# One transformer stack on one core: the convolution's tiles placed anew, sums and copies moved by a step, and the beginning in another order

## The reference, cut to what matters

```python
def modulate(h, shift, scale):
    return h * (1.0 + scale) + shift

def adaln(cond, prm):                       # 72 chunks of 1 MB for both layers
    mod = jax.nn.silu(cond) @ prm["mod_w"] + prm["mod_b"]

def half_ffn(x, m, name):
    sh, sc, g = m
    h = modulate(rms_norm_2(x, prm[name + "_norm"]), sh, sc)
    return x + 0.5 * g * swiglu(h, prm[name + "_w_in"], prm[name + "_w_out"])

def conv_module(u, prm):                    # mixer of b2.0, 512 channels, latent and context apart
    a, g = jnp.split(u + prm["conv_glu_b"], 2, axis=-1)
    y = a * jax.nn.sigmoid(g)
    y = depthwise convolution of y over 31 tokens (15 on each side), + conv_dw_b
    return jax.nn.silu(layer_norm(y, prm["conv_ln_g"], prm["conv_ln_b"]))
```

## Time and profile before

| | |
|---|---|
| time, median of 3 runs | 2585.43 us (2583.7 to 2586.07) |
| profiled execution, its own time | 2585.32 us |
| its span | 2583.5 us |
| TensorE busy | 2494.8 us, 97% |
| VectorE, ScalarE, POOL busy | 1330.1, 986.3, 132.2 us |
| TensorE on the chain that ended last | 90% |
| DMA | 353.13 MB, 137 GB/s |

### The profile page before, as it was taken

The page is one execution under the profiler, slowest core; times in us unless marked ns, Lnnn a source line. Parts: engine busy times, 40 slices in busy tenths (PEclk is TensorE's granted clock), DMA queues, the critical chain, the costliest instruction groups (busy, mean ns, idle before and its releaser), DMA issues.

```text
span 2583.5 us, 39883 instructions
## 1 busy us (share of the span) xinstructions
PE 2494.8 (97%) x16458; PEld 2095.1 (81%) x16458; DVE 1330.1 (51%) x1978; ACT 986.3 (38%) x1482; POOL 132.2 (5%) x161
## 2 busy tenths in 40 slices
PE   7999999999899999999999999999999999988999
PEld 6998899998888888876457788887888887857999
DVE  4567775488753333345764543343443343355654
ACT  4346544366462222251263421223321224345532
POOL 0000000000000000002930000000000000011000
PEclk9999999999999999999999999999999999999999
DMA  5447555454342322332541423224222232533553
GB/s 216 174 150 253 173 177 196 141 183 159 131 163 95 125 82 77 110 115 91 212 173 63 150 95 109 90 97 160 96 95 98 88 116 90 188 131 123 184 192 106
DMA packets 62690, 353.13 MB, mean 137 GB/s; under 512 B 14400, under 2 KB 17600, under 8 KB 26432
## 3 DMA queue, kind: packets, MB, share of 16 engines
q1 hardware_dynamic: 62528, 350.82, 38.9%
HBM read 349.75 MB, written 1.05 MB: 136 GB/s over the span
## 4 chain that ended last, share of the span: by engine, by line
PE 90%; DVE 5%; ACT 2%; DMA 2%; issue 1%; POOL 0%; SPq 0%; DVEq 0%; ACTq 0%; POOLq 0%
PE psum L1251 16%; PE psum L1252 16%; PE psum L1253 16%; PE psum L772 11%; PE psum L809 7%; PE psum L811 6%; PE psum L810 6%; DVE slab L2349 2%; PE psum L884 1%; PE psum L890 1%; PE psum L885 1%; PE psum L1140 1%; DVE ring_lo L2217 1%; PE psum L915 1%; PE psum L917 1%
## 5 line engine op out<-in xcount | busy, mean ns | idle before, releaser
L1251 PE MATMUL psum<-h_hi,w_hi 128*128 128x512 f32 (+1 forms) x1408 | 513.2, 364 | 10.0 <-DVE h_lo L2186 7.8
L1252 PE MATMUL psum<-h_lo,w_hi 128*128 128x512 f32 (+1 forms) x1408 | 511.6, 363 | 0.0
L1253 PE MATMUL psum<-h_hi,w_lo 128*128 128x512 f32 (+1 forms) x1408 | 511.5, 363 | 0.0
L2363 DVE TENSOR_TENSOR w_lo<-wring,w_hi 128x1024 fp32r<-128x1024 f32 (+1 forms) x240 | 318.6, 1330 | 305.0 <-ACT w_hi L1791 304.6
L1791 ACT ACTIVATE w_hi<-wring 128x1024 fp32r<-128x1024 f32 (+1 forms) x240 | 273.3, 1143 | 525.8 <-PE psum L1253 518.4
L809 PE MATMUL psum<-h_hi,w_hi 128*128 128x256 f32 (+1 forms) x1176 | 357.0, 304 | 1.9 <-DVE ring_lo L2217 0.9
L811 PE MATMUL psum<-h_hi,ring_lo 128*128 128x256 f32 (+1 forms) x1176 | 348.5, 296 | 0.0
L810 PE MATMUL psum<-h_lo,w_hi 128*128 128x256 f32 (+1 forms) x1176 | 347.9, 296 | 0.0
L2217 DVE TENSOR_TENSOR ring_lo<-wring,w_hi 128x1024 fp32r<-128x1024 f32 x208 | 246.8, 1223 | 167.7 <-ACT w_hi L1670 165.7
L1251 PEld LDWEIGHTS psum<-h_hi,w_hi 128*128 128x128 f32 x1408 | 266.3, 189 | 54.8 <-issue 8.6
L1253 PEld LDWEIGHTS psum<-h_hi,w_lo 128*128 128x128 f32 x1408 | 266.4, 189 | 41.4
(11 more groups left out here) (203 smaller groups left out, 3451.3 us busy)
## 6 DMA issues: line engine op xcount, KB each, us to landing
wring<-in_w_b_ffn_in SPq DMA_DIRECT2D x84, 1024.0 KB, 4.9
wring<-in_w_mod SPq DMA_DIRECT2D x72, 1024.0 KB, 5.1
wring<-in_w_b_ffn_out SPq DMA_DIRECT2D x64, 704.0 KB, 4.0
wring<-in_w_b_merge SPq DMA_DIRECT2D x24, 1024.0 KB, 4.9
wring<-in_w_b_out SPq DMA_DIRECT2D x16, 1024.0 KB, 4.9
wring<-in_w_b_in SPq DMA_DIRECT2D x16, 1024.0 KB, 5.7
wring<-in_w_b_q SPq DMA_DIRECT2D x12, 1024.0 KB, 4.9
wring<-in_w_b_k SPq DMA_DIRECT2D x12, 1024.0 KB, 4.8
```

The costliest lines, as they stand in the source:

```text
L1251: nc.tensor.matmul(acc, wh[:, k, :], rhs_hi[k], start=(k == 0), stop=False)
L1252: nc.tensor.matmul(acc, wh[:, k, :], rhs_lo[k], start=False, stop=False)
L1253: return nc.tensor.matmul(acc, wl[:, k, :], rhs_hi[k], start=False, stop=(k == n - 1))
L2363: V.tensor_tensor(part_piece(w_lo, q, i), raw_piece(c, i), part_piece(w_hi, q, i).bitcast(F32), ALU.subtract).then_inc(weights_split, 1)
```

## The change

It has six parts.

- **Convolution.** TensorE takes tiles 3 and 0. Four copies of a tile's input, shifted by one token each, stand in four groups of 32 partitions, for 32 channels at a time; 16 DMAs from SBUF to SBUF make them for a tile, on SyncE's queue, 32 x 2 x 284 elements each. One product then does four taps of 32 channels: 8 quads of taps by 4 groups of channels, 32 products with 32 output rows and 512 columns. Their weights are an additional 1 MB chunk ("taps"). VectorE takes tiles 2 and 1, one after the other, POOL none; the buffers of the diagonals go. The order of the chunks around it follows.
- **Context.** Squares, sums and root one chunk later.
- **Attention.** The rows are copied a step earlier than now (their turn a step later, in the last one).
- **Beginning.** x first, then constants, then parameters. The table of the root is loaded at once. The first roundings and splits stand behind root and reciprocal, the silu of the condition behind the first roundings of the input.
- **b2.1.** Six modulation chunks with the heads instead of five, two before ffn2 instead of three, those of the attention at steps 2 to 5 instead of 0 to 3, its two splits two steps later.
- **FFN.** The second input chunk has a name of its own in the plan; only before b2.1.ffn2 does it come earlier, behind the first modulation chunk.

```diff
-DVE_CONV, POOL_CONV = 2, 1
-PE_CONV = DVE_CONV + POOL_CONV
 CONV_ORDER = (3, 0, 2, 1)
+PE_CONV, DVE_CONV = CONV_ORDER[0:2], CONV_ORDER[2:4]
+QUADS = (TAPS + 3) // 4
+REACH = SEQ + 4 * (QUADS - 1)
...
-              ("b2.0.heads", 6), ("b2.0.att", 7), ("b2.0.n2", 3), ("b2.1.n1", 5), ("b2.1.nm", 4), ("b2.1.heads", 5), ("b2.1.att", 4),
-              ("b2.1.n2", 3)]
+              ("b2.0.heads", 6), ("b2.0.att", 7), ("b2.0.n2", 3), ("b2.1.n1", 5), ("b2.1.nm", 4), ("b2.1.heads", 6), ("b2.1.att", 4),
...
+SECOND_AT = {"b2.1.n2": 1}
...
-ROUND_AT = {"b1.0": (KD - 1, KD - 1), "b2.0.n1": (0, 0), "b1.1": (KD - 2, KD - 2), "b2.1.n2": (KD - 2, KD - 2)}
...
+ROUND_AT = {"b1.0": (KD, KD), "b2.0.n1": (0, 0), "b1.1": (KD - 2, KD - 2), "b2.1.n2": (KD - 2, KD - 2)}
...
-        out[i * (steps - 3) // len(MODS[nm]) if nm[1] == "1" else i].append(("mod", l, c))
+        out[i * (steps - 3) // len(MODS[nm]) if nm[1] == "1" else i + 2 * (nm == "b2.1.att")].append(("mod", l, c))
     if MODS[nm]:
-        out[steps - 2].append(("turn", 0, 0))
+        out[steps - 2].append(("rows", 0, 0))
+        out[steps - 1].append(("turn", 0, 0))
...
-        for at, c in ((4, 0), (6, 1)):
+        for at, c in ((6, 0), (8, 1)):
...
-        mods(before)
+        chunks = [(f"mod{m}", 1, KD * 256) for m, _ in MODS[before]]
+        at = SECOND_AT.get(before, len(chunks))
+        plan.extend(chunks[:at] + [(f"{nm}_second", 1, KD * 256)] + chunks[at:])
...
-            mods("b2.0.conv")
-            plan += [("b2.0.in", 2, KD * 256)]
+            taps = [(f"mod{m}", 1, KD * 256) for m, _ in MODS["b2.0.conv"]]
+            plan += taps[0:2] + [("b2.0.taps", 1, len(PE_CONV) * QUADS * P)]
+            plan += [("b2.0.in", 2, KD * 256)] + taps[2:]
             between = [("mod%d" % m, 1, KD * 256) for m, _ in MODS["b2.0.uq"]]
-            plan += [("b2.0.uq", 1, 3 * 384)] + between[0:2] + [("b2.0.uq", 1, 3 * 384)] + between[2:5]
-            plan += [("b2.0.ukv", 1, 2 * 1024)] + between[5:7]
+            plan += [("b2.0.uq", 1, 3 * 384)] + between[0:2] + [("b2.0.uq", 1, 3 * 384)] + between[2:4]
+            plan += [("b2.0.ukv", 1, 2 * 1024)] + between[4:7]
             mods("b2.0.heads")
         else:
             between = [(f"mod{m}", 1, KD * 256) for m, _ in MODS["b2.1.heads"]]
-            plan += [("b2.1.in", 7, KD * 256)] + between[0:2] + [("b2.1.in", 1, KD * 256)] + between[2:]
+            plan += [("b2.1.in", 7, KD * 256)] + between[0:3] + [("b2.1.in", 1, KD * 256)] + between[3:]
...
-            sp.dma_start(prm[:, :], d_param).then_inc(s_first, 16)
-            sp.dma_start(cst[:, 0:EARLY], d_const[:, 0:EARLY]).then_inc(s_first, 16)
             for i in range(2):
                 sp.dma_start(x[:, KH_X * i:KH_X * i + KH_X, 0:SEQ], d_x[:, KH_X * i:KH_X * i + KH_X, :]).then_inc(s_x, 16)
+            sp.dma_start(cst[:, 0:EARLY], d_const[:, 0:EARLY]).then_inc(s_first, 16)
+            sp.dma_start(prm[:, :], d_param).then_inc(s_first, 16)
...
+                for n in range(len(PE_CONV)):
+                    if c == start["b2.0.taps"][0] + n:
+                        for ready in ("b2.0.conv.margin", f"b2.0.conv.glu{PE_CONV[n]}"):
+                            if E.new(ready):
+                                sp.wait_ge(*E.at(ready))
+                        for j in range(4):
+                            w = min(REACH, YW - j)
+                            for g in range(GROUPS):
+                                sp.dma_start(m_shifted[n][GW * j:GW * j + GW, g, :, 0:w],
+                                             m_y[GW * g:GW * g + GW, PE_CONV[n], :, j:j + w]).then_inc(s_shift[n], 16)
...
+            def convolve(n, wv, chunk=None):
+
+                acc = take(f"b2.0.conv.pe{n}", fixed=6).rearrange("p (a s) -> p a s", a=2)
+                pe.wait_ge(s_shift[n], 16 * 4 * GROUPS)
+                for k in range(QUADS):
+                    for g in range(GROUPS):
+                        mm = product(acc[GW * g:GW * g + GW, :, :], wv[:, n, k, GW * g:GW * g + GW], m_shifted[n][:, g, :, 4 * k:4 * k + SEQ],
+                                     k, QUADS)
+                if chunk is not None:
+                    E.name_next(f"w{chunk}")
+                mm.then_inc(tap_multiplied, 1)
+                E.step(tap_multiplied, f"b2.0.conv.pe{n}")
...
-                    if l == 1 and j < 2:
-                        for k in range(4 * j, 4 * j + 4):
+                    if l == 1 and j in (1, 2):
+                        for k in range(4 * j - 4, 4 * j):
...
-                    convolve(MODS["b2.0.conv"])
+                    modulation(*MODS["b2.0.conv"][0])
+                    taps, w = state["c"] + 1, slot_of(state["c"] + 1)
+                    wv = w[:, 0:len(PE_CONV) * QUADS * P].rearrange("p (n k c) -> p n k c", n=len(PE_CONV), k=QUADS)
+                    pe.wait_ge(landed[taps % SLOTS], 16 * (taps // SLOTS + 1))
+                    convolve(0, wv)
+                    modulation(*MODS["b2.0.conv"][1])
+                    state["c"] += 1
...
+                if j == 5:
+                    convolve(1, wv, taps)
+                if j == 6:
+                    modulation(*MODS["b2.0.conv"][2])
...
-                A(warm[:, :], C("eps"), ACT.Sqrt).then_inc(rooted, 1)
-                act.wait_ge(rooted, E.step(rooted))
+                if nm == "b1.0":
+                    A(warm[:, :], csil[:, 0, 0:1], ACT.Sqrt).then_inc(rooted, 1)
+                    act.wait_ge(rooted, E.step(rooted))
...
-                if l == 1:
-                    context_squares()
-                for m in range(8, 10):
-                    round_chunk(last[m])
+                for m in range(2):
+                    if l == 1:
+                        context_squares(range(4 * m, 4 * m + 4))
+                    round_chunk(last[8 + m])
+            context_root()
...
+                        if kind == "rows":
+                            copy_rows(nm)
                         if kind == "turn":
-                            copy_rows(nm)
...
-                if ahead and nm in ROUND_AT:
+                if ahead and nm in ROUND_AT and nm != "b1.0":
...
-            for k in range(TAPS):
-                tap(k)
-                if k == 19:
-                    split_chunk(projections[6])
             rope_pieces("b2.0.lora")
-            glu(2)
-            glu(1)
-            for k in range(TAPS):
-                tap(TAPS + k)
+            split_chunk(projections[6])
+            for i in DVE_CONV:
+                glu(i)
+                for k in range(TAPS):
+                    tap(i, k)
```

121 lines of the change are left out of this document (58 added, 63 removed).

## The result

The changed kernel takes 2558.64 us in the median of four runs (2558.06 to 2559.42), the kernel before 2585.75 beside it: 27.1 us less, a ratio of 0.9892 (0.9877 to 0.9907). I had forecast 2553.1, in 2546 to 2566. So the direction and most of the mechanisms held, and 5.1 of 32.2 us did not come. The profiled execution took 2558.64, its span is 2556.6.

A forecast was written before the change was run, and what follows sets the result against it. TensorE was taken as the bound, busy 2494.8 of 2583.5 us. Mixer −17.0, beginning −3.4, context −4.35, rows and turn −2.1 and last layer −5.4 sum to −32.2: 2585.3 to 2553.1 us, range 2546 to 2566.

The forecast's parts named there:

- The convolution on TensorE: Mixer of b2.0: 27.2 us of diagonal products go, 128 overlapping records cost 15.1 (bounds 14.2 and 56.7), saving 12.1.
- VectorE's taps and the reciprocal: Mixer: 60 taps at 0.796 us end about 1253.5, reciprocal at 1254.5, before TensorE needs it at 1262.0; 3.5 us wait goes.
- I give 0.6 back: Mixer: three modulations instead of two stand behind each other before the attention, at the queue's pace, costing 0.6 us.
- The copies at nothing: Mixer: 32 shifted-copy DMAs on SP's queue land in time and cost nothing; TensorE waits under 1 us for them.
- The beginning: Kernel start: x lands about 0.9 us earlier, root ends at 13.8 instead of 18.03; −3.4 us, bounds −1.5 to −4.5.
- The context: Last output chunks: sums one chunk later remove the wait for ScalarE's squares, −4.35 us; up to 2 may come back.
- Rows and turn: Attentions of two layers: row copy a step earlier, turn a step later; 2 × −1.05 = −2.1 us, bounds 0 and −5.2.
- The last layer: b2.1: later modulations in attention −3.5, a sixth at the heads −1.0, before ffn2 −0.9; together −5.4 us.
- rival D: Gains outside the mixer turn into the next wait, half of 15.2 us gone, 2560.7; chance 0.23.
- A: Convolution on TensorE: the groups do not overlap, 128 records take 56.7 us in line, 2594.7; chance 0.03.
- B: Mixer: VectorE becomes the bound, taps of 1.386 us make the reciprocal late by 28, 2581.1; chance 0.04.
- C: Mixer: shifted copies are late, at an issue of 1.0 us; +6 us, 2559.1; chance 0.15.

The follow-up runs named there:

- the groups in line: Changed kernel with the two loops of TensorE's convolution exchanged, all eight quads of one column group before the next group: 2590.49 us, ratio 1.0006.

## Why the prediction was right, and where it was off

- **The convolution on TensorE: right.** 12.1 forecast; two sets of 6.9 instead of 7.55 give 27.2 − 13.7 = 13.5. The longer records lost nothing at all, they are even below my lower bound of 14.2 for both, since a record of this form takes 0.429 in line and not the 0.443 that I took from the diagonal products. The exchanged loops show that the overlap of groups is the reason. At the changes between the widths little is to be seen: around the second set the records start 0.1 us late ahead of it and 0.14 behind it (1197.08; the last four records of the set start at 1196.51, and 0.43 behind them would be 1196.94), near the 0.3 that I left out; whether that is a drain no run shows.
- **VectorE's taps and the reciprocal: right.** Done before TensorE wants it, 0.786 a tap, and slow again as soon as POOL works.
- **"I give 0.6 back" for the chunks at the heads: the term that failed.** 3.8 came back. I had counted the pace of the queue (2.5 us a chunk) and overlooked what stands ahead of it. The chunk ukv holds its slot until 1247.5, and the three modulations behind it theirs, so from 1230.7 to 1247.6 SyncE loads nothing. Before, there was a gap of 19 us too (1255.3 to 1274.2), under the 3.54 of the reciprocal. A stall had hidden a stall: with POOL kept busy the reciprocal is late again, and the waits for chunks are gone. Fewer and later modulations there took them away for good, in two kernels.
- **The copies at nothing:** 1.1 in the first profile and 0.3 in the second, where I had allowed 1. The first set was issued 0.1 behind the GLU and took 10.33 where I had 9.9, and its last copy landed 4.0 later. The load of in5 behind it was not late.
- **The beginning: the mechanism right, x's landing mis-sized.** I took 0.9 for asking first; it is 2.7 at the first product. The rest, 3.5 by the run with constants first, was 2.5 in my sum (3.4 − 0.9). Together they are 6.2, outside my bound of 4.5: the first product starts at 16.31, where I had 19.1.
- **The context: right, and worth 7.25 to 7.5 instead of 4.35**, as TensorE ran the products behind the wait at half its clock in both profiles of before.
- **Rows and turn: right** (1.1 and 0.85 for 1.05 each).
- **The last layer: a size off.** −2.4 to −3.5 for −5.4. The attention gave 1.4 to 1.8 for 3.5, since ScalarE's and POOL's waits took the rest, as rival D had it. The new places ahead of the FFN gave 0.6 or 0.7 for 0.9, and this is no more than the modulation of 1.0 that went to the heads.
- **Not forecast: the clock.** From 1300 to 2240 the changed kernel lost 3.3 to 3.4 us in both profiles, where nothing but the copy of the rows in one attention was moved; 2.7 to 3.0 of it stand at the lower clock.
- **Errors that cancel.** Convolution, context and beginning gave some 6 to 8 us more than forecast, the heads, the copies, the last layer and the stretch from 1300 to 2240 some 10 less. That the sum is only 5.1 off is in part luck.

Of the rivals, A is refuted by the trace, and B did not come because POOL rests; the runs with the groups in line and with POOL kept busy show that both are real where their condition holds. C's condition, an issue of 1.0 us, was not met; the 1.1 came from a late landing. D is what happened in the last layer, and within the mixer, where it had not been looked for, at the heads.

## What to carry to other kernels

Narrow float32 products cost a quarter (0.107 us a record instead of 0.429) if neighbours go to four different column groups, and most of that is lost (0.35) if the same products stand in the other loop order. Before a wait is counted as gain, ask which other wait ends just under it: here a reciprocal's 3.5 us had covered the gap of a ring whose slots one long-lived chunk held. And look at the clock behind a wait before you price it: at the context it made 7.25 of 4.35. The reverse holds as well: waits can look short because TensorE runs slowly under them, as ahead of the last FFN, so time such a place from end to end.

## What the runs showed of the hardware that was not expected

- In each of the 14 profiles TensorE lost 16 to 32 us of engine time in stretches in which its clock stood at the lower of its two levels (0.50 of 2.4 GHz, so 1.2). Some stretches come back at the same work: the one behind the wait at the context in both profiles of the kernel before, and one at the start of the last FFN in eight of nine profiles with its new places and in none of five with those of before. Others move between profiles of one kernel. They do not need a wait in front: in the first profile of the changed kernel the clock fell at 494.3 behind 10 us in which TensorE was busy throughout, and in the second profile it stayed at full speed there.

```profile
484.00:494.00 10.00, 10.00 (x58) 8.72 (x57) 4.44 (x5) 2.98 (x4) 0.00 (x0) 1.00 0.33 124
494.30:501.10 6.80, 6.80 (x26) 5.59 (x26) 4.06 (x10) 3.29 (x5) 0.00 (x0) 0.50 0.47 154
```

  The Trainium skill (TensorE: Matmul & The Clock Gate, Part 1: The HAM clock gate) says of a kernel's start that the count of slow products varies from run to run, since the gate's window runs freely. The profiles agree as far as they show the same kernel with slow stretches in other places, five new and three gone between the first two. What draws a slow stretch stays open.
- A slow stretch costs from nearly all of its lost share to nearly nothing: 1.5 us of 1.7 in the first attention (+0.4 against −1.1 from 290 to 330), and 0.2 to 0.9 of some 3 at the last FFN, where waits get shorter by it.
- A 128x512 tap of VectorE takes 0.786 us alone and 1.27 to 1.39 beside POOL's work on other data. The Trainium skill (GPSIMD Engine Reference, Specifications) says that POOL's SBUF interfaces are shared with VectorE and that they contend when VectorE's instruction has two SBUF inputs. The trace agrees, and adds the size.
- Small copies from SBUF to SBUF cost the issuing queue 0.6 us each, as the 64 KB loads did, and land in 2.1, where those took 2.7.
